# Two decoder layers in split fp32: the low halves of the weights move from VectorE to GpSimd

## The reference, cut to what matters

```python
def hybrid_layer(h, norm_g, w_in, ...):
    xn = rms_norm(h, norm_g)
    proj = xn @ w_in                       # 2048 -> 5376 columns
    qa, fa, ia, ga, qb, kb, vb, gb, uc, gc = jnp.split(proj, splits, axis=-1)
    ya = rms_norm(hgrn2_mixer(qa, fa, ia, lb, valid), hgrn_norm_g)      # 4 heads of 128, gated recurrence
    yb = swa_sink_attention(rope(qb), rope(kb), vb, sinks)              # 16 heads of 64, window 128
    yc = multiscale_pool(uc, valid, pool_w, pool_scale)                 # windows 2, 4, 8, 16
    mixed = jnp.concatenate([ya * jax.nn.silu(ga), yb * jax.nn.silu(gb), yc * jax.nn.silu(gc)], axis=-1)
    return h + mixed @ w_out               # 2048 -> 2048
```

## Time and profile before

| what | value |
|---|---|
| median of 3 runs | 1633.53 us (1633.40 to 1633.59) |
| span of the profiled execution, first to last instruction | 1632.0 us |
| PE busy | 1612.1 us, 99% |
| DVE busy | 915.2 us, 56% |
| ACT busy | 645.5 us, 40% |
| POOL busy | 20.8 us, 1% |
| granted TensorE clock | 1.00 throughout |
| DMA moved | 147.23 MB, 90 GB/s |

### The profile page before, as it was taken

One profiled execution on the slowest core, in us unless ns is written; L12 is line 12 of the kernel. 1 busy time (PEld: TensorE's weight loads), 2 busy tenths in 40 slices (PEclk: granted clock), 3 DMA queues, 4 the chain that ended last, 5 costly groups with the idle time before them and its releaser, 6 DMA issues.

```text
span 1632.0 us, 27854 instructions
## 1 busy us (share of the span) xinstructions
PE 1612.1 (99%) x11366; PEld 1493.0 (91%) x11366; DVE 915.2 (56%) x1897; ACT 645.5 (40%) x1280; POOL 20.8 (1%) x78
## 2 busy tenths in 40 slices
PE   6999999999999999999999999999999999999999
PEld 6999999999999999999998899889999988888887
DVE  7677877645666554434335678774555674443231
ACT  7676455423222432323237764553223233232121
POOL 0000000000000000000000000000000000000000
PEclk9999999999999999999999999999999999999999
DMA  6222210112121223344432221112111212234441
GB/s 251 79 104 78 79 53 29 51 53 78 57 74 62 94 80 115 124 138 135 140 118 79 103 78 66 39 52 78 53 68 63 79 52 103 104 121 137 145 147 48
DMA packets 28014, 147.23 MB, mean 90 GB/s; under 512 B 3568, under 2 KB 3696, under 8 KB 12656
## 3 DMA queue, kind: packets, MB, share of 16 engines
q1 hardware_dynamic: 27888, 145.46, 25.8%
HBM read 136.86 MB, written 8.52 MB: 89 GB/s over the span
## 4 chain that ended last, share of the span: by engine, by line
PE 96%; DVE 2%; issue 1%; ACT 0%; DMA 0%; SPq 0%; DVEq 0%
PE ps_gemm L816 80%; PE ps_mix L706 3%; PE ps_mix L742 3%; PE ps_mix L658 2%; PE ps_mix L672 2%; PE ps_mix L701 1%; PE ps_gemm L634 1%; DVE rstd L900 1%; PE ps_mix L786 1%; PE ps_mix L788 0%; PE ps_mix L718 0%; PE ps_mix L775 0%; PE ps_mix L737 0%; DVE w_lo L883 0%; DMA w_stage<-in_w_in 0%
## 5 line engine op out<-in xcount | busy, mean ns | idle before, releaser
L816 PE MATMUL ps_gemm<-x_hi,w_hi 128*128 128x264 f32 (+1 forms) x2304 | 561.7, 311 | 12.5 <-DVE w_lo L883 10.3
L816 PE MATMUL ps_gemm<-x_hi,w_lo 128*128 128x264 f32 (+1 forms) x2304 | 543.1, 304 | 0.0
L816 PE MATMUL ps_gemm<-x_lo,w_hi 128*128 128x264 f32 (+1 forms) x2304 | 542.6, 303 | 0.0
L816 PEld LDWEIGHTS ps_gemm<-x_hi,w_hi 128*128 128x128 f32 x2304 | 371.1, 189 | 32.9 <-DVE w_lo L883 11.1
L816 PEld LDWEIGHTS ps_gemm<-x_hi,w_lo 128*128 128x128 f32 x2304 | 370.8, 189 | 16.5
L816 PEld LDWEIGHTS ps_gemm<-x_lo,w_hi 128*128 128x128 f32 x2304 | 370.2, 189 | 14.4
L883 DVE TENSOR_TENSOR w_lo<-w_stage,w_hi 128x512 fp32r<-128x512 f32 x464 | 305.5, 689 | 104.0 <-ACT w_hi L440 92.7
L440 ACT ACTIVATE w_hi<-w_stage 128x512 fp32r<-128x512 f32 x464 | 265.3, 618 | 169.7 <-DVE z L960 122.7
L816 PE MATMUL ps_gemm<-mixed_hi,w_lo 128*128 128x264 f32 (+1 forms) x768 | 205.2, 322 | 0.0
L816 PE MATMUL ps_gemm<-mixed_lo,w_hi 128*128 128x264 f32 (+1 forms) x768 | 205.0, 321 | 0.0
L816 PE MATMUL ps_gemm<-mixed_hi,w_hi 128*128 128x264 f32 (+1 forms) x768 | 203.9, 320 | 0.0
(11 more groups left out here) (169 smaller groups left out, 1407.1 us busy)
## 6 DMA issues: line engine op xcount, KB each, us to landing
w_stage<-in_w_in SPq DMA_DIRECT2D x83, 1024.0 KB, 4.8
w_stage<-in_w_out SPq DMA_DIRECT2D x32, 1024.0 KB, 4.8
x_in<-in_xT SPq DMA_DIRECT2D x4, 1056.0 KB, 9.8
res<-in_xT SPq DMA_DIRECT2D x16, 264.0 KB, 3.0
h1T<-z SPq DMA_DIRECT2D x16, 264.0 KB, 3.4
res<-h1T SPq DMA_DIRECT2D x16, 264.0 KB, 3.0
out<-z SPq DMA_DIRECT2D x16, 256.0 KB, 3.2
rope<-in_c_rope SPq DMA_DIRECT2D x2, 528.0 KB, 3.6
```

The costliest lines, as they stand in the source:

```text
L816: ins = pe.matmul(g[:, bank, 0:size], ws[:, N % 2, tick], xs[:, k, c:c + size], start=tick == 0 and i == 0, stop=tick == TICKS - 1 and i == 2)
```

## The change

For all blocks but block 0, the subtraction `w_low(N, q)` is issued by GpSimd and no longer by DVE. Its shape and place in memory are the same. On GpSimd it waits, as on DVE, for the quarter's `w_hi`, and at a block's first quarter also for PE to have finished block `N - 2`. DVE keeps the four subtractions of block 0, with a semaphore of their own, `s_wlo0`; so `s_wlo` counts from block 1 on, and the waits of SP and PE are renumbered. GpSimd's program is written anew, tick by tick: the memset of `a_vmeta` at the last tick of a layer's first block, `w_low(N + 1, q)` at ticks 2, 5, 8 and 11, and the copies of the meta columns at the ticks of the exponentials. The instructions of ACT do not change, and those of PE only in their semaphore waits.

```diff
+        s_wlo0 = sem("w_lo_done_first_chunk")
...
         @block.sync
             def load_w(N):
 
-                if N >= 2:
-                    sp.wait_ge(s_wlo, 4 * (N - 1))
+                if N == 2:
+                    sp.wait_ge(s_wlo0, 4)
+                elif N > 2:
+                    sp.wait_ge(s_wlo, 4 * (N - 2))
...
         @block.gpsimd
         def _(pool):
-            for layer in range(DEPTH):
-                if layer:
-                    pool.wait_ge(s_gemm, NC * layer)
-                else:
-                    pool.wait_ge(s_xlo, 16)
-                    pool.wait_ge(s_xsq, 16)
-                pool.memset(vm[:], 0.0).then_inc(s_avz, 1)
-                for q in range(len(ATT_B[layer])):
-
-                    Q = ATT_Q0[layer] + q
-                    nq = N_META if ATT_B[layer][q][0] == 0 else P
-                    if Q >= 2:
-                        pool.wait_ge(s_amt, Q - 1)
-                    for pair in range(2):
-                        heads = slice(2 * pair, 2 * pair + 2)
-                        pool.wait_ge(s_aex, 4 * Q + 2 * pair + 2)
+            def w_low(N, q):
+
+                pool.wait_ge(s_whi, 4 * N + q + 1)
+                if N >= 2 and q == 0:
+                    pool.wait_ge(s_gemm, N - 1)
+                part = (slice(None), N % 2, slice(4 * q, 4 * q + 4))
+                pool.tensor_tensor(wl[part], wst[part], wh[part].bitcast(F32), ALU.subtract).then_inc(s_wlo, 1)
+
+            for N in range(NTOT):
+                layer, n = divmod(N, NC)
+                for tick in range(TICKS):
+                    if n == 0 and tick == TICKS - 1:
+                        if layer:
+                            pool.wait_ge(s_gemm, NC * layer)
+                        else:
+                            pool.wait_ge(s_xlo, 16)
+                            pool.wait_ge(s_xsq, 16)
+                        pool.memset(vm[:], 0.0).then_inc(s_avz, 1)
+                    if tick in HI_TICKS and N + 1 < NTOT:
+                        w_low(N + 1, HI_TICKS.index(tick))
+                    at = att_at(layer, n, tick, EXP_LAG)
+                    if at and at[1] % 2 == 1:
+
+                        q, i = at
+                        Q = ATT_Q0[layer] + q
+                        nq = N_META if ATT_B[layer][q][0] == 0 else P
+                        heads = slice(i - 1, i + 1)
+                        if Q >= 2 and i == 1:
+                            pool.wait_ge(s_amt, Q - 1)
+                        pool.wait_ge(s_aex, 4 * Q + i + 1)
                         pool.tensor_copy(pmc[0:nq, Q % 2, heads], pr[0:nq, Q % 2, heads, AT_META:AT_CUR])\
                             .then_inc(s_apm, 1)
...
         @block.tensor
-                    if tick % 4 == 0:
-                        pe.wait_ge(s_wlo, 4 * N + tick // 4 + 1)
+                    if tick % 4 == 0 and N == 0:
+                        pe.wait_ge(s_wlo0, tick // 4 + 1)
+                    elif tick % 4 == 0:
+                        pe.wait_ge(s_wlo, 4 * (N - 1) + tick // 4 + 1)
...
         @block.vector
-            def w_low(N, q):
-
-                dve.wait_ge(s_whi, 4 * N + q + 1)
-                part = (slice(None), N % 2, slice(4 * q, 4 * q + 4))
-                dve.tensor_tensor(wl[part], wst[part], wh[part].bitcast(F32), ALU.subtract).then_inc(s_wlo, 1)
+            def w_low_first(q):
+
+                dve.wait_ge(s_whi, q + 1)
+                part = (slice(None), 0, slice(4 * q, 4 * q + 4))
+                dve.tensor_tensor(wl[part], wst[part], wh[part].bitcast(F32), ALU.subtract).then_inc(s_wlo0, 1)
...
                 if k % 4 == 0:
-                    w_low(0, k // 4)
+                    w_low_first(k // 4)
...
-                    if tick - 1 in HI_TICKS and N + 1 < NTOT:
-                        w_low(N + 1, HI_TICKS.index(tick - 1))
```

## The result

The changed kernel takes **1681.35 us** (median of 4 runs, 1679.27 to 1684.71), the kernel before beside it 1633.56 (4 runs, 1633.40 to 1633.89): 47.8 us more, a ratio of **1.0294 (1.0282 to 1.0306)**. The direction and the mechanism were the forecast's; the time lies 5 us above the range's end of 1676. The mean granted clock of its four executions was 0.991 to 0.994. The profiled one was the slowest, 1684.71 us, so its span is 50.9 us longer than before, where the medians differ by 47.8.

A forecast was written before the change was run, and what follows sets the result against it. TensorE was taken to bound the kernel. Heads +24.4, start +2.5 and attention +1 gave +28 on a span of 1632.0, so 1660, and a median of 1661.5 us, range 1640 to 1676.

The forecast's parts named there:

- What bounds, and the exchange of turns: Whole kernel: TensorE bounds; GpSimd and DVE instructions reading SBUF exclude each other and take turns; 0.63.
- The price of a pass: One `w_lo` subtraction on GpSimd: 1.1 us, between bounds of 0.53 and 1.6.
- Term 1: Second half of each head's recurrence: DVE's chain held by three passes, TensorE starts 2.9 us later.
- Term 2: Beginning of each head: L1128 held until a pass ends, +0.3 us net of 1.0.
- Term 3: Last head of each layer: passes fall over the gate's split and next chain, +2.3 us, and +0.3 from term 2.
- The sum of the heads: All eight heads' recurrences: six by 3.2 and two by 2.6, +24.4 us.
- Term 4: The start: block 1's first passes hold the last `x_lo` and the sums, +2.5 us.
- Term 5: Attention: only single coincidences reach TensorE, +1 us for both layers, 0 to 4; pooling and other blocks 0.
- (a): Rival: DVE is not held by long GpSimd passes; only existing waits go, -2.8 us, 1630.7; chance 0.15.
- (b): Rival: GpSimd lets nothing in between its queued passes; +4.1 instead of 2.9 per head, 1671 us; chance 0.12.
- (c): Rival: DVE keeps the reads through its chain, so only the first hold counts; +10, 1643 us; chance 0.10.
- The range: Whole kernel: 1640 to 1676 us, taking in (b), (c) and a pass price from 0.53 to about 1.4.

The follow-up runs named there:

- experiment 5: Changed kernel with each GpSimd subtraction replaced by two memsets of `w_lo` (writes only, low halves left out): 1632.11 us, 0.9991.
- experiment 6: Changed kernel with each GpSimd subtraction replaced by a copy of `w_stage` to `w_lo` (one read): 1639.22 us, 1.0034.
- experiment 7: Kernel before, with GpSimd making only the low halves in blocks 10 to 20 of each layer (pooling and attention): 1642.82 us, 1.0059.
- experiment 1: Changed kernel with the subtractions of the recurrence's blocks (21 to 32 of each layer) back on DVE: 1644.12 us, 1.0063.
- experiment 3: Kernel before, with 14 tiny DVE additions ahead of one step's L1165 in each of the six full heads, nothing moved to GpSimd: 1655.71 us.
- experiment 2: Changed kernel, all 460 subtractions still on GpSimd, but paced by the recurrence's steps in each head's first two blocks: 1645.23 us, 1.0067.
- experiment 8: Kernel before, with block 31's four passes per layer on GpSimd, paced, and early `w_lo` reordered at the start: 1630.86 us, 0.9982.

## Why the prediction was wrong in size

- **What bounds, and the exchange of turns: right.** TensorE bounds, DVE's shorter work is worth nothing to it, and the waits named are there, once per head ahead of the recurrence's step. The Trainium skill, "SBUF — State Buffer", section "Who interferes with whom", says that a DVE instruction with two SBUF inputs contends with a GpSimd one that reads SBUF and not with one that only writes it. Experiments 5 and 6 bear out both halves: 434 ns beside memsets, 506 beside copies, 1.38 us in the chain beside a subtraction.
- **The price of a pass, 1.1 us: low.** It is 1.257 at least and 1.296 in the median (1.378 in the mean, with DVE's turns in it), within the bounds of 0.53 and 1.6. The estimate of 1.12 from the Trainium skill, "GPSIMD Engine Reference", section 3, was low by as much.
- **Term 1: the mechanism right, the size by luck.** L1165, L1166 and L1168 took 1.28, 1.43 and 1.38, PE waited 2.68 (2.9 was said). Two errors cancel here. With passes of 1.3 the forecast's own working gives 0.6 more, 3.5. But it let each instruction begin only when the pass had ended, and each pass only when the instruction had; in the rows the 0.43 us instructions add 0.1 to 0.2 to the 1.3 of a pass, since the two engines' work overlaps in part. The period of the head whose clock stayed at 1.00 was 51.95 us (51.7 was said).
- **Term 2: right that L1128 is held** (1.54 us, 0.99 more than before, in the group of the heads of layer 0), and nearly all of it is covered: PE waits for L1131 once, 0.2 us.
- **Term 3: right.** The last heads cost 2.8 and 3.1 (2.6 said); PE waits twice in each, 0.75 and 1.72, then 0.87 and 1.79.
- **The sum of the heads: 24.4 said. 38.1 came, of which 11.8 is clock.** Without it 26.3 is left. **This is the step that failed: the sum priced the wait and had no term for what PE does after it.** The prediction does not mention the granted clock; the table of the kernel before has it at 1.00 throughout, and the sum took that for a constant. But the earlier trace rows show no wait of PE over 1.6 us behind the first matmuls, so that trace could not say what a wait of 2.9 would do to it. An unknown cost was put at nothing without a reason. 11.8 us more puts the forecast at 1673, inside its range, and the 8.2 us by which the next failed step was short put it at 1681.5. The profiled execution's 1684.7 holds 1.9 more in the heads and 1.5 of a drift that is told in the last section.
- **Term 4: 2.5 said, 2.0 came**, the waits for `x_lo` up from 0.9 to 2.6.
- **Term 5: 1 said (0 to 4), 9.2 came by the take-outs, 9.1 by experiment 7.** The second failed step is its clause that the blocks for pooling have "whole blocks or several us of reserve". Pooling is a chain (L1035, L1036, L1037, L632) with some 0.3 us before PE: waits of 1.43 and 2.63, and a slow stretch behind the second (1.8 by the sum of 1 - clock, 1.5 in time by experiment 1). The 9.2 and the 9.1 agree partly by chance: only the first has the clock in it. The attention scores' own 2.2 us of waits are in the forecast's 0 to 4. The clause "each collision there would cost up to 1.1" was also short: a chain of three is three collisions.
- **Rivals.** (a) falls by L1168's 1.38 us; experiment 5 shows what it takes to make it true. (b) falls: three DVE instructions run within four passes. (c) falls: L1166 and L1168 are held as L1165 is.
- **The range.** Its upper end of 1676 came from rival (b) and from a price of about 1.4 us. At the measured 1.30 the forecast's own sums would give some 36 us, or 1670, so the price alone did not leave the range; what lay outside was the clock and the pooling.

## What to carry to other kernels

Moving work to an idle engine is free only if the two do not shut each other out: compare what they read, and look at each short dependent chain on the old engine, where a 0.18 us instruction can cost 1.2 us, as many times as there are links. Where a chain of turns can meet the bounding engine, pace the moved work by the chain's own semaphores: that gave back 36 of 48 us here. And price a wait of TensorE of some 2.4 us or more with what can follow it: one piece of delay cost 7.9 us more in six heads than the same delay in two, 6.0 of it by the clock.

## What was not expected of the hardware

- **The clock after a wait.** After waits of 2.41 to 2.70 us, TensorE ran at 1.2 instead of 2.4 GHz for up to 6.8 us, at a cost of 1.5 to 3.1 us; after waits of 1.03, 0.89, 1.72 and 1.79 it did not. Nor did it after each of the long ones: the wait of 2.69 that ended at 1269.83 was followed by eight matmuls in 0.97 us and a window at 1.00, the wait of 2.63 in experiment 7 had no fall either where the same wait in the change had one, and three of the six waits of 2.41 in experiment 3 had none. What tells them apart was not tried and stays open.
- **What each stream costs on GpSimd**, for 128x512 elements: 0.53 us to fill, 0.62 to copy, 1.30 to subtract, all in the median. The first read costs 0.09, the second 0.68.
- **A fill holds a one-input instruction too**: L1128 0.55 alone, 0.76 beside fills, 0.85 beside copies, 1.54 beside subtractions, while two-input instructions do not feel a fill at all. The same section of the Trainium skill says that DVE's two-port modes contend with GpSimd, whichever issues first holding the pair; these rows agree, if L1128 runs in such a mode, which is inferred from its rate (528 elements in 0.55 us, against 0.71 for L1131) and not shown.
- **A drift not explained.** In the 24 blocks behind layer 0's heads the median period was 11.75 us instead of 11.68 in the profiled execution of the change and in that of experiment 5, and 11.68 in those of experiments 1, 2, 6, 7 and 8. It comes with memsets as with subtractions, and stays away with both kinds of load, so it seems to be one of an execution and not of the kernel: 1.5 us in one. In experiment 5 the profiled execution took 1633.93 us and the other nine 1632.0 to 1632.2.
